# Interleaving the slots of two expert tiles by retrieval rounds in a hybrid encoder layer on one Trainium2 core

## The chip, the cores and the metric

The kernel runs on one core of one Trainium2 chip. The metric is the device time of one execution in microseconds. The median of three runs of the kernel before is 1806.68 us (1801.11 to 1808.39).

## The reference

One layer of a streaming encoder for 640 tokens of 1024 channels: 128 tokens of eight running streams and 512 of a prompt, all in float32. In the kernel these are five tiles of 128 tokens; tile 0 holds the running streams, tiles 1 to 4 the prompt. After the mixing front (a gMLP half and an RG-LRU half), each token asks for experts:

```python
q = (xb @ w_q).reshape(PEER_BLOCK, PEER_HEADS, 2, D_HALF)      # 8 heads, 2 halves of 128
s1 = einsum("thd,kd->thk", q[:, :, 0], k1); s2 = einsum("thd,kd->thk", q[:, :, 1], k2)
v1, i1 = top_k(s1, 16); v2, i2 = top_k(s2, 16)
cand = v1[..., :, None] + v2[..., None, :]                     # best 16 of the pair sums
top_s, sel = top_k(cand, 16); eidx = take_along_axis(cidx, sel); g = softmax(top_s)
act = gelu(einsum("thkd,td->thk", u_tab[eidx], xb))
y = einsum("thk,thkd->td", g * act, v_tab[eidx])
```

So each token has 8 x 16 = 128 experts out of 16384, each a row of u_tab (1024 numbers) and one of v_tab. The host lays the two tables side by side as `experts`, 8 KB a row. The result is added to x, and a last RMSNorm gives y.

## The kernel before, in words

**A slot** is one expert for each of a tile's 128 tokens: one indirect DMA of POOL. The sparse tiles 0, 3 and 4 gather whole rows, u and v (1 MB a slot). For the dense tiles 1 and 2 only u rows are gathered (0.5 MB, `udot`), and their v part is a product with the whole v table: two table passes over it, each of 64 blocks of 128 rows (0.5 MB, loaded by SP at L585). Before each pass a filling builds the matrix of coefficients `cm` of the pass for all 256 dense tokens, in 32 batches of 8 tokens: VectorE compares (`one_hot`, L1030 and L1032), ScalarE scales (L1296), TensorE multiplies (`fill`, L1556), ScalarE copies (L1304). The pass is `add_block`, L1567.

**A whole slot** goes: gather (L631), dot with h2 on VectorE (`dot`, L969), gelu and coefficient on ScalarE (L1266, L1270). Then its v row is added: either on TensorE, with a diagonal made by ScalarE (L1277) and four matmul records into accY (`weigh`, L1582), or on VectorE (`add_v`, L989). `by_vector` (L181) says which. Tile 3 is on TensorE in its first 64 slots, tile 4 in three of five; both are on VectorE in the other 64, which run beside a table pass. `take` (L1050) adds accY to the tile, after its last slot.

**The ring** has six places of 8 KB per partition, twelve half places for u rows. POOL issues the gathers in the order of the dots (`GATHERS`), each after the ring place's last user is done (`freed`) and, at each new retrieval round, after `idx_ready` (L625).

**Retrieval.** The queries of tiles 3 and 4 are made in 8 rounds, one head each (`Q` items, L1500); ScalarE keeps them (L1261). A round then goes in steps x: scores on TensorE at x = 5r + 4, best keys at 5r + 5 and 5r + 6, pair sums at 5r + 7, second eight at 5r + 8, numbers and weights at 5r + 9, all but the scores on VectorE (L840 to L959). A round gives 16 slots to each of the two tiles.

**The order** of all engines is one list, `ORDER`. `weave` (L87) gives each item a due number and sorts by it; each engine walks the list and executes its part in that order. Due numbers are about microseconds of the plan, not measured ones. After the dots of tile 0 and the u rows of tile 1 come the front of tiles 3 and 4 beside the u rows of tile 2, then filling and pass with tile 3, then filling and pass with tile 4. `adopt` (L999) makes h2 of the next tile, `ids` and `prep` bring the dense tiles' numbers and coefficients to the layout of the filling, `flush` (L1042) adds a pass's result, `norm` and `square_y` are the last RMSNorm.

## Time and profile before

| | |
|---|---|
| median of three runs | 1806.68 us |
| those runs, lowest and highest | 1801.11, 1808.39 us |
| profiled execution, span | 1799.8 us (its time with what lies around the span is not listed) |
| TensorE busy | 1455.5 us, 81% |
| VectorE busy | 1429.5 us, 79% |
| ScalarE busy | 634.6 us, 35% |
| POOL busy | 801.6 us, 45% |
| DMA | 675.75 MB, mean 375 GB/s |
| whole-slot gathers, u gathers | 384, 256 |
| dots L969 | 466.4 us in 384, 1222 ns each |
| adds on VectorE L989 | 238.3 us in 186, 1281 ns each |

The page's busy shares are means over stages with different limits. The slices (40 of 45 us) show the stages; the windows, groups, waits and timelines below are of the same execution. A busy time counts an instruction from start to end, and neighbours overlap a little: where a cost is wanted, the distance between starts is the better measure.

### The profile page before, as it was taken

The numbers are of one execution on the slowest core, as the hardware profiler recorded it, in microseconds if no ns is written. First come the engines' busy times: TensorE is split into PE (matmuls) and PEld (weight loads), VectorE is DVE, ScalarE is ACT, GpSimd is POOL, SyncE is SP. The second block draws the span as 40 slices with busy tenths as digits, with TensorE's granted clock in tenths as the row PEclk, the third lists the DMA queues.
The fourth block names the chain that finished last, engine by engine and source line by source line (L and its number), as shares of the span: only waits on it lengthen the run. The fifth ranks groups of instructions, "written<-read, shape, count | busy, mean of one in ns | idle before, by whom it ended". The sixth has DMA issues, their size and how long they took to land.

```text
span 1799.8 us, 16917 instructions
## 1 busy us (share of the span) xinstructions
PE 1455.5 (81%) x4706; PEld 790.5 (44%) x4706; DVE 1429.5 (79%) x3050; ACT 634.6 (35%) x1936; POOL 801.6 (45%) x667
## 2 busy tenths in 40 slices
...
GB/s 355 155 342 409 384 358 402 341 396 398 408 398 410 379 415 397 386 342 392 405 304 307 353 345 362 418 416 417 416 417 352 371 351 375 388 417 417 417 417 283
DMA packets 146478, 675.75 MB, mean 375 GB/s; under 512 B 15216, under 2 KB 15472, under 8 KB 97232
## 3 DMA queue, kind: packets, MB, share of 16 engines
...
HBM read 671.61 MB, written 3.01 MB: 375 GB/s over the span
## 4 chain that ended last, share of the span: by engine, by line
DMA 28%; PE 27%; DVE 16%; issue 10%; POOL 9%; ACT 8%; ACTq 0%; DVEq 0%; POOLq 0%; SPq 0%
DMA ring<-experts,idc 19%; DMA arena<-experts 9%; PE accY L1582 8%; POOL ring L633 8%; PE pb L1567 5%; PE pb L1373 4%; DVE ring L969 3%; DVE ring L980 3%; PE pb L1382 2%; PE pb L1556 2%; ACT arena L1296 2%; POOL ring L631 2%; DVE xt L989 2%; DVE arena L1030 2%; PE pb L1391 1%
## 5 line engine op out<-in xcount | busy, mean ns | idle before, releaser
L631 POOL DMA_INDIRECT ring<-experts,idc x384 | 462.7, 1205 | 844.4 <-DVE xt L989 373.6
L969 DVE CUSTOM_DVE_ANT_0 ring<-ring,h 128x1024 f32<-128x1024 f32 x384 | 466.4, 1222 | 198.0 <-DMA ring<-experts,idc 196.7
L1582 PE MATMUL accY<-ring,diag 128*128 128x512 f32 x792 | 450.4, 704 | 197.0 <-ACT diag L1277 197.0
L1567 PE MATMUL pb<-arena 128*128 128x512 f32 x1024 | 472.4, 606 | 19.7 <-DMA arena<-experts 13.1
L633 POOL DMA_INDIRECT ring<-experts,idc x256 | 328.7, 1284 | 110.5 <-issue 76.3
L1266 ACT ACTIVATE ge<-zt 128x1 f32<-128x1 f32 x384 | 76.4, 199 | 757.8 <-DVE zt L969 756.4
L1582 PEld LDWEIGHTS accY<-ring,diag 128*128 128x128 f32 x792 | 157.6, 216 | 402.9 <-ACT diag L1277 275.0
L1567 PEld LDWEIGHTS pb<-arena 128*128 128x128 f32 x1024 | 186.1, 191 | 304.4 <-issue 197.4
L989 DVE SCALAR_TENSOR_TENSOR xt<-ring,coef,xt 128x1024 f32<-128x1024 f32 x186 | 238.3, 1281 | 14.2 <-ACT coef L1270 13.9
L980 DVE CUSTOM_DVE_ANT_0 ring<-ring,h 128x1024 f32<-128x1024 f32 x128 | 151.7, 1222 | 8.3 <-DMA ring<-experts,idc 7.2
L1296 ACT ACTIVATE arena<-arena,qT 128x64 f32<-128x64 f32 x512 | 129.1, 334 | 81.2 <-DVE arena L1032 81.2
L980 DVE CUSTOM_DVE_ANT_0 ring<-ring,arena 128x1024 f32<-128x1024 f32 x128 | 153.2, 1221 | 5.5 <-DMA ring<-experts,idc 4.7
L1500 PE MATMUL pq<-arena 128*128 128x256 f32 (+1 forms) x736 | 147.6, 359 | 7.3 <-ACT arena L1261 3.9
L1556 PEld LDWEIGHTS pb<-arena 128*128 128x128 f32 x1024 | 131.3, 201 | 41.7 <-issue 31.2
L1500 PEld LDWEIGHTS pq<-arena 128*128 128x128 f32 x736 | 128.0, 199 | 32.7 <-issue 18.6
L1556 PE MATMUL pb<-arena 128*128 128x64 f32 x1024 | 127.6, 280 | 4.8 <-ACT arena L1296 4.8
L1270 ACT ACTIVATE coef<-ge,gc 128x1 f32<-128x1 f32 x384 | 113.1, 295 | 12.6
L1030 DVE TENSOR_TENSOR arena<-iota,qT 128x1024 f32<-128x1024 f32 x64 | 78.2, 1222 | 20.7 <-PE pb L1556 20.7
L1277 ACT ACTIVATE diag<-ident,coef 128x128 f32<-128x128 f32 x198 | 79.5, 402 | 6.4
L1363 PE MATMUL pb<-ident,arena 128*128 128x128 f32 x100 | 18.5, 355 | 72.8 <-ACT arena L1124 52.2
L1373 PE MATMUL pb<-arena 128*128 128x256 f32 (+1 forms) x384 | 72.7, 352 | 2.9 <-ACT arena L1131 2.9
L1382 PE MATMUL pb<-arena 128*128 128x512 f32 x144 | 66.1, 616 | 6.3 <-ACT arena L1173 6.3
...
## 6 DMA issues: line engine op xcount, KB each, us to landing
arena<-experts SPq DMA_DIRECT2D x128, 512.0 KB, 15.0
...
ring<-experts,idc POOLq DMA_INDIRECT x640, 9.5
...
```

The source lines that it names most:

```text
L631: nc.gpsimd.indirect_dma_start(ring[:, at // 2], None, experts, index).then_inc(gat[at], 16)
L633: nc.gpsimd.indirect_dma_start(half(g), None, halves, index).then_inc(gat[at], 16)
L969: V.tensor_tensor_reduce(out=half(g), in0=half(g), in1=h2[:], scale=1.0, scalar=0.0, op0=ALU.mult, op1=ALU.add, accum_out=zt[:, s % 8:s % ...
L980: V.tensor_tensor_reduce(out=half(g), in0=half(g), in1=h, scale=1.0, scalar=0.0, op0=ALU.mult, op1=ALU.add, accum_out=zd[:, u:u + 1]).then ...
L989: V.scalar_tensor_tensor(out=x, in0=ring[:, PLACE["whole", s][0] // 2, D:2 * D], scalar=coef[:, s % 8:s % 8 + 1], in1=x, op0=ALU.mult, op1 ...
L1030: V.tensor_tensor(hot2[:, k % 2], iota[:].unsqueeze(1).to_broadcast([P, BATCH, P]), idT[:, 1, a].unsqueeze(2).to_broadcast([P, BATCH, P]), ...
L1296: ins = A.activation(hot1[:, k % 2, i], hot1[:, k % 2, i], ACT.Copy, scale=idT[:, 2, n * BATCH + i:n * BATCH + i + 1])
L1373: ins = T.matmul(pflat[:, o:o + w], wt[:, c, m * P:(m + 1) * P], hT[:, c, 0:w], start=c == 0, stop=c == DC - 1)
L1500: ins = T.matmul(out, wt[:, c, o:o + P], h2T[:, c, 0:w], start=c == 0, stop=c == DC - 1)
L1556: ins = T.matmul(pb[:, k % 4, i * BLOCKS:(i + 1) * BLOCKS], hot2[:, k % 2, i], hot1[:, k % 2, i], start=True, stop=True)
L1567: ins = T.matmul(pb[:, 2 * j + k], cm[:, i, j * P:(j + 1) * P], vring[:, n % VRING, k * 512:(k + 1) * 512], start=i == 0, stop=i == BLOCKS ...
L1582: ins = T.matmul(accY[:, j], diag[:, (n - 1) % DIAGS], ring[:, place, D + j * 512:D + (j + 1) * 512], start=first, stop=final)
```

## The change

The slots of tiles 3 and 4 no longer run tile by tile. `slot_order` lists them: 24 of tile 3 (the tail) between the last u rows and a little beyond; the first filling with 54 (24 of tile 3, 30 of tile 4); the first pass with 62 (18 of tile 4, 44 of tile 3); the second filling with 54 (36 of tile 3, 18 of tile 4); the second pass with 62 of tile 4. In the tail all slots are on TensorE, in the fillings four of five, in the passes none. Rounds 0 to 2 of the retrieval are due in the tail's stretch, rounds 3 to 7 all in the first pass. Tile 3's h2 lies in a tensor of its own, h3, in the place of the gate weights, so that both tiles can be dotted in any order; tile 4's is made in h2 after the last u row. The accumulation on TensorE is cut into runs of one tile (`RUNS`): a take stands after each run, and the next run's first weighing waits for it. There are five runs where there were three. The last RMSNorm's square is an item of its own, since a tile is complete only after its last slot. `adds_before` and `takes_before` count adds ahead of takes and takes ahead of adds, for their waits.

```diff
-SPARSE = [0, 3, 4]
+TAIL, FILLED, BLOCKED = 24, 54, 62
+
+def slot_order():
+
+    third = [(3, k) for k in range(SLOTS)]
+    fourth = [(4, k) for k in range(SLOTS)]
+    tail = third[0:24]
+    fill0 = third[24:48] + fourth[0:30]
+    block0 = fourth[30:48] + third[48:92]
+    fill1 = third[92:128] + fourth[48:66]
+    block1 = fourth[66:128]
+    assert (len(tail), len(fill0), len(block0), len(fill1), len(block1)) == (TAIL, FILLED, BLOCKED, FILLED, BLOCKED)
+    return [(0, k) for k in range(SLOTS)] + tail + fill0 + block0 + fill1 + block1
+
+SLOT = slot_order()
+WHOLE = len(SLOT)
+
+def stretch(s):
+
+    at = s - SLOTS - TAIL
+    if at < 0:
+        return ("first", s) if s < SLOTS else ("tail", s - SLOTS)
+    half, at = divmod(at, FILLED + BLOCKED)
+    return ("fill", at) if at < FILLED else ("block", at - FILLED)
+
+def by_vector(s):
+
+    kind, i = stretch(s)
+    if kind == "first":
+        return i < SLOTS // 2 and i % 2 == 1
+    return kind == "block" or (kind == "fill" and i % 5 == 3)
+
+ON_PE = [sum(not by_vector(k) for k in range(s + 1)) for s in range(WHOLE)]
+ON_DVE = [s + 1 - ON_PE[s] for s in range(WHOLE)]
+LAST_SLOT = {t: max(s for s in range(WHOLE) if SLOT[s][0] == t) for t in (0, 3, 4)}
+
+def runs_on_pe():
+
+    runs = []
+    for s in range(WHOLE):
+        if not by_vector(s):
+            if not runs or SLOT[runs[-1][-1]][0] != SLOT[s][0]:
+                runs.append([])
+            runs[-1].append(s)
+    return runs
+
+RUNS = runs_on_pe()
+RUN_OF = {s: g for g, run in enumerate(RUNS) for s in run}
...
             u += 1
     b += 0.6
     put.append((b + 2.02, ("take", 0)))
+    put.append((b + 2.03, ("square", 0)))
...
     for r in range(HEADS):
         for part in range(3):
-            put.append((b + 55.04 + 0.9 * (3 * r + part), ("Q", r, part)))
-    for x in range(4, 10):
-        put.append((b + 58.08 + 2.6 * (x - 4), ("II", 2, x)))
+            put.append((b + 55.04 + 1.2 * (3 * r + part), ("Q", r, part)))
+    c = b + 55.0
+    for x in range(4, 20):
+        put.append((c + 3.58 + 2.2 * (x - 4), ("II", 2, x)))
+    put.append((c + 6.11, ("adopt", 3)))
+    s = SLOTS
+    for n in range(TAIL):
+        put.append((c + 15.61 + 1.2 * n, ("dot", s + n)))
+        put.append((c + 16.72 + 1.2 * n, ("mix", s + n)))
     while u < DTOK:
-        b += 0.6
-        put.append((b, ("udot", u)))
-        u += 1
-    b += 1.0
-
-    for x in range(10, rounds_steps(2)):
-        r, k = divmod(x - 10, 5)
-        put.append((b - 3 + 16 * r + 2.7 * k + 0.07, ("II", 2, x)))
+        wide = 1.2 if b < c + 14 else 2.4
+        for _ in range(2):
+            put.append((b, ("udot", u)))
+            u += 1
+        b += wide
     put.append((b - 12.01, ("ids",)))
-    put.append((b + 0.02, ("adopt", 3)))
     put.append((b + 0.2, ("prep",)))
-    s = SLOTS
+    put.append((b + 0.4, ("adopt", 4)))
+
+    b = c + 15.61 + 1.2 * TAIL
+    s += TAIL
+    taken = 1
     for h in range(2):
-        for n in range(64):
+        hot = (FILLED - 2) / BATCHES
+        for n in range(FILLED):
             put.append((b + 0.1 + n, ("dot", s + n)))
             put.append((b + 1.11 + n, ("mix", s + n)))
         for n in range(BATCHES):
-            put.append((b + 1.5 + 1.9 * n, ("hot", h, n)))
-            put.append((b + 3.55 + 1.9 * n, ("fill", h, n)))
-        b += 64
-        for n in range(64):
-            put.append((b + 0.1 + 1.5 * n, ("dot", s + 64 + n)))
-            put.append((b + 1.61 + 1.5 * n, ("mix", s + 64 + n)))
+            put.append((b + 0.5 + hot * n, ("hot", h, n)))
+            put.append((b + 2.45 + hot * n, ("fill", h, n)))
+        for g, run in enumerate(RUNS):
+            if g >= taken and s <= run[-1] < s + FILLED:
+                put.append((b + 1.61 + run[-1] - s, ("take", g)))
+                taken = g + 1
+        if h == 1:
+            put.append((b + 4.0 + LAST_SLOT[3] - s, ("square", 3)))
+            put.append((b + 7.02 + LAST_SLOT[3] - s, ("norm", 3)))
+        b += FILLED
+        s += FILLED
+        wide = 1.5 * BLOCKS / BLOCKED
+        for n in range(BLOCKED):
+            put.append((b + 0.1 + wide * n, ("dot", s + n)))
+            put.append((b + 1.61 + wide * n, ("mix", s + n)))
         for n in range(BLOCKS):
             put.append((b + 0.7 + 1.5 * n, ("block", h, n)))
+        if h == 0:
+            for x in range(20, rounds_steps(2)):
+                put.append((b + 1.33 + 2.6 * (x - 20), ("II", 2, x)))
         b += 96
-        s += SLOTS
+        s += BLOCKED
         if h == 0:
-            put.append((b + 0.05, ("adopt", 4)))
-            put.append((b + 0.4, ("take", 3)))
             put.append((b + 1.3, ("flush", 0)))
-            put.append((b + 5.02, ("norm", 3)))
-    put.append((b + 2.0, ("take", 4)))
+    put.append((b + 2.0, ("square", 4)))
     put.append((b + 2.1, ("norm", 4)))
     put.append((b + 2.2, ("flush", 1)))
     put.append((b + 2.3, ("norm", 1)))
...
-def by_vector(s):
-
-
-    t, k = divmod(s, SLOTS)
-    if t == 0:
-        return k < SLOTS // 2 and k % 2 == 1
-    return k >= SLOTS // 2 or (t == 2 and k % 5 in (1, 3))
-
-
-WHOLE = len(SPARSE) * SLOTS
-ON_PE = [sum(not by_vector(k) for k in range(s + 1)) for s in range(WHOLE)]
-ON_DVE = [s + 1 - ON_PE[s] for s in range(WHOLE)]
...
         ws = sb("ws", [GROUPS, P])
-        wab = sb("wab", [HC, P])
-        wib = sb("wib", [HC, P])
+        wabi = sb("wabi", [2 * HC, P])
+        wab = wabi[:, 0:HC]
+        wib = wabi[:, HC:2 * HC]
+        h3 = wabi[:].rearrange("p m n -> p (m n)")
...
+            known = 0
             for g in GATHERS:
                 kind, s = g
                 at, _, lay = PLACE[g]
-                t, k = SPARSE[s // SLOTS] if kind == "whole" else DENSE[s // SLOTS], s % SLOTS
+                t, k = SLOT[s] if kind == "whole" else (DENSE[s // SLOTS], s % SLOTS)
                 f = FRONT_OF[t]
                 per = SLOTS // ROUNDS[f]
-                if k % per == 0 or (f == 0 and k == TOPK):
-                    first = f == 0 and k == 0
-                    pool.wait_ge(idx_ready, 1 if first else ROUND_BASE[f] + k // per + 2)
+                ready = 1 if f == 0 and k < TOPK else ROUND_BASE[f] + k // per + 2
+                if ready > known:
+                    pool.wait_ge(idx_ready, ready)
                     pool.sem_inc(pool_held, 1)
+                    known = ready
                 if lay:
                     freed(pool, lay)
...
             def dot(s):
-                g = "whole", s
-                if s % SLOTS == 0:
-                    v.wait_ge(h2_ready, H2_TILES.index(SPARSE[s // SLOTS]) + 1)
+                g, t = ("whole", s), SLOT[s][0]
+                if all(tile != t for tile, _ in SLOT[:s]):
+                    v.wait_ge(h2_ready, H2_TILES.index(t) + 1)
-                V.tensor_tensor_reduce(out=half(g), in0=half(g), in1=h2[:], scale=1.0, scalar=0.0, op0=ALU.mult,
...
             def add_v(s):
-                t = SPARSE[s // SLOTS]
-                x = xt[:, X_PLACE[t]]
+                x = xt[:, X_PLACE[SLOT[s][0]]]
                 v.wait_ge(coefs, s + 1)
+                if s and TAKES_AT_ADD[s] and by_vector(s):
+                    v.wait_ge(y_taken, TAKES_AT_ADD[s])
...
                 if t == 4:
-                    v.wait_ge(dots, 2 * SLOTS)
-                V.scalar_tensor_tensor(out=h2[:], in0=xt[:, X_PLACE[t]], scalar=rs_ffn[:, t:t + 1], in1=g_ffn[:],
+                    v.wait_ge(udots, DTOK)
+                V.scalar_tensor_tensor(out=h3 if t == 3 else h2[:], in0=xt[:, X_PLACE[t]], scalar=rs_ffn[:, t:t + 1], in1=g_ffn[:],
                                        op0=ALU.mult, op1=ALU.mult).then_inc(h2_ready, 1)
...
-            def take(t):
-                n = SPARSE.index(t)
-                x = xt[:, X_PLACE[t]]
-                v.wait_ge(vdone, ON_PE[SLOTS * (n + 1) - 1])
-                v.wait_ge(vadds, ON_DVE[SLOTS * (n + 1) - 1])
+            def take(g):
+                x = xt[:, X_PLACE[SLOT[RUNS[g][-1]][0]]]
+                v.wait_ge(vdone, ON_PE[RUNS[g][-1]])
+                v.wait_ge(vadds, ADDS_AT_TAKE[g])
                 V.tensor_tensor(x, x, accY[:].rearrange("p a b -> p (a b)"), ALU.add).then_inc(y_taken, 1)
...
             def square_y(t):
                 n = LAST.index(t)
-                a.wait_ge(y_taken, n + 1)
+                if t in DENSE:
+                    a.wait_ge(y_taken, len(RUNS) + DENSE.index(t) + 1)
+                else:
+                    a.wait_ge(y_taken, max(g for g, run in enumerate(RUNS) if SLOT[run[-1]][0] == t) + 1)
+                    a.wait_ge(vadds, ON_DVE[LAST_SLOT[t]])
...
-                n, k = ON_PE[s], s % SLOTS
-                first = k == 0
-                final = not any(not by_vector(o) for o in range(s + 1, s - k + SLOTS))
-                if first and s:
-                    t.wait_ge(y_taken, s // SLOTS)
+                n, run = ON_PE[s], RUN_OF[s]
+                first, final = s == RUNS[run][0], s == RUNS[run][-1]
+                if first and run:
+                    t.wait_ge(y_taken, run)
```

## Rows read from the trace of the kernel before

**Rows 1.** The page, slices: GB/s that DMA moved in each of 40 slices.
```profile
GB/s 355 155 342 409 384 358 402 341 396 398 408 398 410 379 415 397 386 342 392 405 304 307 353 345 362 418 416 417 416 417 352 371 351 375 388 417 417 417 417 283
```

**Rows 2.** Windows: busy us (instructions) of each engine, then PEclk, DMA share, GB/s.
```profile
855.00:919.00 64.00, 52.26 (x235) 44.10 (x234) 60.32 (x172) 7.52 (x14) 41.27 (x33) 0.95 1.00 387
919.00:1115.00 196.00, 178.46 (x799) 110.18 (x800) 179.54 (x444) 146.26 (x509) 81.52 (x62) 0.97 0.89 332
1115.00:1357.00 242.00, 231.59 (x516) 93.33 (x514) 184.57 (x347) 41.74 (x147) 66.55 (x65) 0.99 1.02 414
1357.00:1545.00 188.00, 153.76 (x681) 99.36 (x681) 166.07 (x222) 125.23 (x457) 88.45 (x63) 0.88 0.94 359
1545.00:1799.80 254.80, 236.61 (x514) 92.24 (x512) 163.53 (x202) 37.34 (x138) 58.06 (x60) 0.99 0.96 393
```

**Rows 3.** Timeline of VectorE: start us, duration us, line, operation.
```profile
891.66 0.50 DVE L840 MAX8 best<-pick 128x8 f32<-128x136 f32 x2
...
894.99 1.22 DVE L980 CUSTOM_DVE_ANT_0 ring<-ring,h 128x1024 f32<-128x1024 f32 x1
...
899.57 1.22 DVE L901 TENSOR_REDUCE e<-pick 128x64 f32<-128x1024 f32 x1
...
901.23 1.22 DVE L980 CUSTOM_DVE_ANT_0 ring<-ring,h 128x1024 f32<-128x1024 f32 x1
...
908.10 0.50 DVE L840 MAX8 vals<-psc 128x8 f32<-128x128 f32 x2
...
910.59 1.21 DVE L980 CUSTOM_DVE_ANT_0 ring<-ring,h 128x1024 f32<-128x1024 f32 x1
...
925.87 0.19 DVE L860 TENSOR_TENSOR pick<-vals 128x32 f32<-128x32 f32 x1
...
928.14 1.22 DVE L969 CUSTOM_DVE_ANT_0 ring<-ring,h 128x1024 f32<-128x1024 f32 x1
...
929.28 1.22 DVE L1030 TENSOR_TENSOR arena<-iota,qT 128x1024 f32<-128x1024 f32 x1
...
931.02 1.22 DVE L969 CUSTOM_DVE_ANT_0 ring<-ring,h 128x1024 f32<-128x1024 f32 x1
```

**Rows 4.** The same, at the start of the second filling.
```profile
1364.83 2.35 DVE L1042 TENSOR_TENSOR xt<-xt,pb 128x1024 f32<-128x1024 f32 x2 [4.88 <-PE pb L1567]
...
1369.98 1.28 DVE L989 SCALAR_TENSOR_TENSOR xt<-ring,coef,xt 128x1024 f32<-128x1024 f32 x1
```

**Rows 5.** Waits in the first filling: us in total, times, longest.
```profile
DVE arena L1030 <- PE pb L1556: 11.9, 7, 3.1
```

**Rows 6.** Waits in the second filling, 1375 to 1545 us.
```profile
PE accY L1582 <- ACT diag L1277: 23.9, 11, 3.6
...
DVE arena L1030 <- PE pb L1556: 8.8, 6, 2.2
...
DVE xt L989 <- ACT coef L1270: 4.7, 8, 0.7
```

**Rows 7.** Timeline of TensorE in the first filling.
```profile
1005.43 3.65 PE L1582 MATMUL accY<-ring,diag 128*128 128x512 f32 x8
1008.92 1.89 PE L1556 MATMUL pb<-arena 128*128 128x64 f32 x16
```

**Rows 8.** Groups of VectorE from 855 to 919 us: count, busy, mean ns.
```profile
L980 DVE CUSTOM_DVE_ANT_0 ring<-ring,h 128x1024 f32<-128x1024 f32 x36 | 42.6, 1221 | 3.2 <-DMA ring<-experts,idc 2.9
```

**Rows 9.** Timeline at the first gather of the kernel.
```profile
98.70 0.17 DVE L933 SCALAR_TENSOR_TENSOR idc<-e 128x16 int32<-128x16 f32 x1
...
109.28 1.23 DVE L969 CUSTOM_DVE_ANT_0 ring<-ring,h 128x1024 f32<-128x1024 f32 x1
```

**Rows 10.** Timeline of TensorE: one query round of tiles 3 and 4.
```profile
861.61 7.14 PE L1500 MATMUL pq<-arena 128*128 128x256 f32 x32 [0.78 <-ACT arena L1261]
```

**Rows 11.** Timeline of ScalarE: back from Sqrt to Gelu.
```profile
1361.61 1.28 ACT L1266 ACT_TABLE_LOAD   x1
...
1362.90 0.20 ACT L1266 ACTIVATE ge<-zt 128x1 f32<-128x1 f32 x1
```

29 lines of the change are left out of this document (24 added, 5 removed).

## The prediction

> **What bounds the kernel now.** I read the page's slices first. DMA moves about 417 GB/s in the two stretches of five slices or so that are the table passes, and 303 to 376 GB/s in most slices of the two stretches that are the fillings [rows 1]. So the ceiling here is 417 GB/s: the whole traffic, 675.75 MB by the page, would take 1620 us at it, and the span is 1799.8 us. The kernel loses 180 us in which DMA isn't full. Then I cut the end of the run by stage [rows 2]: u rows of tile 2 (855 to 919 us), filling of tile 3 (919 to 1115), first pass (1115 to 1357), filling of tile 4 (1357 to 1545), second pass and end (1545 to 1799.8). The passes run at 414 GB/s and, with the end in it, 393; the fillings at 332 and 359. At 417 GB/s a whole slot (1.049 MB) costs 2.515 us, a u row half of it, 1.257, a block of the table 1.257. A filling of 64 slots needs 161 us of DMA; the first takes 196 and the second 188. These 35 and 27 us are what the change can win; the 91 us or so lost before 855 us it leaves alone.
>
> What holds the fillings is VectorE, in its order. From starts of neighbouring instructions [rows 3]: a dot takes 1.14 to 1.15 us, a pair of one-hots 1.74, and one retrieval round 2 x 2.49 (best keys) + 2.27 (sums) + 3.33 + 1.66 = 12.2 us; a vector add 1.28 at most [rows 4]. First filling: 64 x 1.147 + 32 x 1.74 + about 3.5 rounds x 12.2 = 73 + 56 + 43 = 172, busy 180 of 196. Second: 73 + 56 + 26 adds x 1.2 + 5 for take, norm and flush = 165, busy 166 of 188 [rows 2]. There the rest are short waits: one-hots for TensorE's filling 8.8 us, adds for their coefficient 4.7 [rows 6]; in the first filling the former are 11.9 [rows 5]. TensorE needs 3.49 / 2 = 1.745 us for a slot, start to start, and for a batch of filling 1.89 less an overlap of 0.16, 1.73 [rows 7]: 112 + 55 = 167 us in the first filling, 66 + 55 = 121 in the second.
>
> **The change, stage by stage.** Up to c, the point 92 u rows into tile 2, nothing in the order moves but the squares' name. 36 u rows run in 855 to 919 [rows 8], so c is at 855 us on VectorE.
>
> (1) From c to the first tail slot. Round 0 now ends (x 9) at due c + 14.58, after 24 u rows; two more u rows and the first tail dot (c + 15.61) follow. VectorE: 24 x 1.147 + 12.2 + 1.3 for adopting tile 3 = 41 us, so the numbers are ready at about 896. But the gathers are issued in the order of the dots by a queue that waits in line: the gather of tail slot 0 needs idx_ready of round 0, and its ring slot is free 12 half slots earlier, at due c + 8.6. From there to the numbers VectorE has 8 u rows and x 7 to 9: 9.2 + 7.3 = 16.5 us in which POOL, and all u gathers behind it, is held. This is a new wait. What is in flight (at most the ring's twelve half places; I estimate 9 u rows, 9 x 1.257) drains in about 12 us of it; then DMA is idle for some 5 us and 2 more until bytes flow: 7 us lost (bounds: 0 if weight pieces fill the hole, 16.5). The nearest row for what follows is the kernel's first gather: from idc at 98.70 to the first dot at 109.28 are 10.6 us with six gathers queued [rows 9]. The first tail dot is thus at about 906.
>
> By the Trainium skill (DMA: Bandwidth & Descriptors, Anatomy of one DMA) a gather takes some 2.0 us plus its bytes at 436 GB/s, 4.4 us here, so an estimate by it would put that dot 5 us earlier; the row differs, and it decides.
>
> (2) The tail: 24 slots with 10 u rows, rounds 1 and 2, ids, prep and the adoption of tile 4. VectorE: 34 x 1.147 + 24.4 + 4 = 67.5. DMA: 24 x 2.515 + 10 x 1.257 = 73, begun at 898. TensorE: 24 x 1.745 = 42, and of the eight query rounds only 0 to 4 stand ahead of the first tail weighing in its order; 5 to 7 come between them at 7.14 + 0.78 = 7.92 us each [rows 10], 24 us, and scores and turns 4: 70. All three would end at 971 to 976. They are coupled through six ring slots, so I add 4: the tail ends at **979** (970 to 990). Against the kernel before, 24 slots and their 60 us of DMA are out of the fillings.
>
> (3) First filling, now 54 slots, no rounds, 11 adds on VectorE. DMA 54 x 2.515 = 136. VectorE 61.9 + 55.7 + 11 x 1.2 + 2 takes 2.4 = 133. TensorE 43 x 1.745 + 55.4 = 130. ScalarE was busy 125 us in the second filling [rows 2], with as many batches, 10 more slots and 5 fewer diagonals: again some 125. Nothing is late by itself, but four queues within 8% of each other don't run without gaps: the stalls of [rows 5, 6] stay. I take 11.9 for one-hots (as where TensorE was as full as here), 2 for 11 adds, 3 for each take in the middle (VectorE waits for TensorE's last weighing of the run, and TensorE's first of the next for y_taken; no row shows it; 0 to 4). That is 133 + 17 = **150 us** (139 to 165). Of 196 before, 46 go, but 10 slots' worth, 25, return in the tail.
>
> (4) First pass: 62 slots, 64 blocks. DMA 62 x 2.515 + 64 x 1.257 = 236. The five rounds 3 to 7 lie here. Before, the last rounds already ran in this pass at 414 GB/s [rows 2]. VectorE: 62 x (1.147 + 1.28) + 61 = 212, under 236, so rounds cost next to nothing; if that cover went they would cost up to 61. Numbers of round 3 come at slot 7 and their first slot is gathered at slot 12. Of 242 before, two slots (5) go and 1 comes: **238** (236 to 250).
>
> (5) Second filling: as the first, but with the wait for TensorE's end of the pass (4.9 us [rows 4]), flush, square and norm of tile 3 in its middle. VectorE 61.9 + 55.7 + 13.2 + 2.4 + 1.5 + 2.3 = 137; stalls 17 + 4.9: **158** (147 to 172). The square's Sqrt takes two table loads, one 1.28 us [rows 11]: 4 us on ScalarE in the middle of work that has only 10 free; contained in that range.
>
> The Trainium skill (ScalarE: Activation LUTs, What ACT_TABLE_LOAD costs) adds a drain of 1.38 us to the load's 1.28, an estimate of 2.8 us more for the two; in the trace the Gelu starts at 1362.90, right behind its load [rows 11], so the load agrees and no drain is seen.
>
> (6) Second pass and end: 254.8 less two slots, 5, less the last take, 1: **249** (247 to 253).
>
> Sum: 979 + 150 + 238 + 158 + 249 = 1774 us of span, 26 less than 1799.8. The time around the span isn't shown on the page; the median of the three runs, 1806.68, is 6.9 above the span, and I keep that distance: 1781, said as **1780 us**.
>
> **Rivals.**
> A, the fillings run at DMA's pace: stalls hide in the ring, since now DMA is the longest queue. For it: in the second filling DMA already ran at 359 with VectorE 2% over it. Then no loss at the hold, 971 + 139 + 238 + 143 + 249 = 1740, time 1747.
> B, slower: TensorE becomes the bound of the fillings. It had 38 weighings to 32 batches in the second filling and still waited 23.9 us for the diagonal [rows 6], with its clock at 0.88 [rows 2]; with 43 in a shorter filling the same 0.63 us per weighing (27) and the same clock (130 / 0.88 = 148) give 175 a filling: 979 + 175 + 238 + 182 + 249 = 1823, time 1830. It decides once the two fillings together pass 334 us. Against it: in the first filling TensorE, busy 178 of 196, held 0.97 of the clock [rows 2].
> C, no gain: the hold of POOL comes with every round (0, 1, 2), not only the first, and each costs DMA 10 us: 1774 + 20 = 1794, time 1801. Against it: round 1 is due 2 slots ahead of its gather's turn, and round 2 further.
>
> **Chances.** Forecast 0.5; A 0.26; C 0.12; B 0.12. The range is to hold 8 in 10: it reaches down to A's time, about which half of A lies above, and up over C's 1801, **1746 to 1808**. A measurement of this kernel can tell about 0.5%, 9 us, from no change. Faster by more than that (under 1797.6): the forecast, A and a little of C, 0.77; within it 0.11; slower (over 1815.7) 0.12.
>
> **What would show it.** The GB/s row of the page should lie at 370 or more through the fillings, and the fillings last 150 and 158 us. Rounds 3 to 7 (L843, L901) should stand inside the first pass, with DMA still at 410 or more. Around 890 us a POOL gather should wait some 15 us for idc, with a dip in GB/s. In fillings the waits of the one-hots (L1030 before) for TensorE should be 10 us or so each, those of a take 1 to 4. Step 4 is wrong if the first pass exceeds 250; step 3 if TensorE's waits for the diagonal pass 25 us in a filling. The prediction fails as a whole if DMA loses time before 855 us, which I hold unchanged.

## The result, and the profile after

The kernel after the change takes 1820.1 us (median of 11 runs, 1808.3 to 1826.43); the kernel before, on the same chips, 1807.64 us (11 runs, 1798.14 to 1810.19). The ratio is 1.0072, with an interval from 1.0054 to 1.0089: slower by 0.7%, where 1780 us and a range up to 1808 us had been forecast. The profiled execution has a span of 1818.7 us, 18.9 longer than the one before (12.5 by the medians), and 44.7 longer than the 1774 us of the sum.

The page's slices of the kernel after, GB/s that DMA moved in each of 40 (45.5 us each); they answer to [rows 1]:

```profile
GB/s 350 154 356 408 378 379 402 339 393 395 408 392 411 387 411 357 395 328 405 310 388 395 345 338 326 380 416 406 387 414 408 330 367 327 351 418 417 417 416 255
```

The two table passes are the runs of slices from 387 to 418. Before the first come a slice of 310 (POOL is held in it), two of 388 and 395 (the tail) and four of 326 to 380 (the first filling); the second filling's four stand at 327 to 367. In the fillings 370 or more had been named as the mark of a right forecast. The windows by stage, with the columns of [rows 2]: c to the first tail dot, the tail of 24 slots, first filling, first pass, second filling, second pass and end.

```profile
855.00:906.00 51.00, 34.46 (x151) 28.58 (x149) 45.48 (x119) 5.53 (x10) 24.18 (x24) 0.87 0.84 325
906.00:988.00 82.00, 69.39 (x213) 39.56 (x214) 67.87 (x199) 31.62 (x91) 42.40 (x35) 0.96 0.98 385
988.00:1158.00 170.00, 146.94 (x686) 95.66 (x684) 132.88 (x185) 118.42 (x439) 73.65 (x54) 0.93 0.91 344
1158.00:1404.00 246.00, 233.72 (x549) 104.08 (x549) 214.78 (x505) 50.84 (x168) 96.21 (x63) 0.96 1.01 408
1404.00:1570.00 166.00, 146.38 (x683) 96.09 (x683) 130.61 (x181) 118.53 (x430) 74.25 (x53) 0.91 0.92 337
1570.00:1818.70 248.70, 234.79 (x511) 92.92 (x509) 163.82 (x196) 36.35 (x134) 60.48 (x58) 0.99 0.94 386
```

Set against the sum: the first tail dot was forecast at 906 us and stands at 906.13. The tail takes 82 us instead of 73, the first filling 170 instead of 150, the first pass 246 instead of 238, the second filling 166 instead of 158, the end 248.7 instead of 249. The differences are +9, +20, +8, +8 and 0, together the 45 us. In the two fillings VectorE is busy 133 and 131 us, close to its forecast work (133 and 137), and idle for the rest; DMA runs at 344 and 337 GB/s. So the work was counted nearly rightly, and the stalls weren't.

Where VectorE idles in the first filling (988 to 1158 us) is told by the groups of its lines: count, busy us, mean ns, then idle time ahead of them with what ended it.

```profile
L1120 DVE TENSOR_TENSOR arena<-iota,qT 128x1024 f32<-128x1024 f32 x32 | 39.1, 1223 | 24.5 <-PE pb L1649 24.5
L1058 DVE CUSTOM_DVE_ANT_0 ring<-ring,h 128x1024 f32<-128x1024 f32 x31 | 37.1, 1220 | 1.1 <-DMA ring<-experts,idc 1.1
...
L1079 DVE SCALAR_TENSOR_TENSOR xt<-ring,coef,xt 128x1024 f32<-128x1024 f32 x10 | 12.8, 1282 | 1.8 <-ACT coef L1359 1.8
...
L1139 DVE TENSOR_TENSOR xt<-xt,accY 128x1024 f32<-128x1024 f32 x2 | 2.4, 1220 | 8.8 <-PE accY L1674 8.8
```

The one-hots of L1120 wait 24.5 us for the filling matmuls of L1649; the two takes of L1139 wait 8.8 us for TensorE's weighings (1.7 us the one in the middle, 7.2 us the one at the filling's end); dots lose 3.2 us to gathers and adds 1.8 to coefficients. The sum of all idle rows is 38.3 us, and 131.7 + 38.3 = 170. The waits of both fillings (us in total, times, longest), first filling first, then two rows of the second:

```profile
PE accY L1674 <- ACT diag L1366: 21.6, 14, 2.5
...
DVE arena L1120 <- PE pb L1649: 22.8, 13, 4.0
PE accY L1674 <- ACT diag L1366: 19.5, 11, 3.0
```

And the same view over the whole run:

```profile
DVE arena L1120 <- PE pb L1649: 47.3, 27, 4.1
...
DVE xt L1139 <- PE accY L1674: 19.5, 4, 7.8
```

The one-hots waited 20.7 us in 13 places in the whole run before (its two fillings are in [rows 5, 6]); now it is 47.3 in 27.

The hold of POOL, as timelines (start us, duration us): the last gather ahead of it and the first tail gather on POOL, then the numbers and the first tail dot on VectorE.

```profile
880.54 0.94 POOL L722 DMA_INDIRECT ring<-experts,idc  x1 [0.30 <-issue]
900.11 1.44 POOL L720 DMA_INDIRECT ring<-experts,idc  x1 [18.63 <-DVE idc L1036]
...
899.11 0.19 DVE L1036 SCALAR_TENSOR_TENSOR idc<-e 128x32 int32<-128x32 f32 x1
...
906.13 1.23 DVE L1058 CUSTOM_DVE_ANT_0 ring<-ring,wabi 128x1024 f32<-128x1024 f32 x1 [4.24 <-issue]
```

POOL stands 18.63 us for the numbers of L1036 (16.5 forecast). The dot follows 7.0 us behind the numbers, where [rows 9] had 10.6, and 6.0 us behind the gather that starts at 900.11. By the Trainium skill (DMA: Bandwidth & Descriptors, Anatomy of one DMA) this gather would take an estimated 4.4 us; the 6.0 us of this row lie between that and the row I had chosen, and decide.

In the tail (906 to 988 us) the waits are these:

```profile
POOL ring L720 <- PE accY L1674: 33.8, 17, 5.5
...
DVE ring L1058 <- DMA ring<-experts,idc: 11.8, 11, 1.9
...
DVE ring L1058 <- issue: 4.2, 1, 4.2
```

POOL waits 33.8 us for weighings to free a ring slot, while VectorE waits for gathered data: the coupling through six slots for which I had added 4 us.

### The profile page after: what moved, and what is told of

The parts are those of the page before. It is cut to its first block, busy times and chain, and to the rows that moved or that the text cites. A ratio compares the mean times of both kernels' runs of the same rounds, so it can differ in the third digit from the quotient of the medians.

```text
span 1818.7 us, 16965 instructions
## 1 busy us (share of the span) xinstructions
PE 1472.1 (81%) x4738; PEld 810.7 (45%) x4738; DVE 1426.7 (78%) x3044; ACT 637.3 (35%) x1944; POOL 832.4 (46%) x667
## 4 chain that ended last, share of the span: by engine, by line
PE 31%; DMA 20%; DVE 18%; issue 12%; ACT 10%; POOL 9%; ACTq 0%; DVEq 0%; POOLq 0%
DMA ring<-experts,idc 11%; PE accY L1674 11%; DMA arena<-experts 9%; POOL ring L722 7%; PE pb L1660 5%; DVE ring L1058 4%; PE pb L1466 4%; PE pb L1649 3%; ACT arena L1385 3%; PE pb L1475 2%; DVE ring L1069 2%; DVE xt L1079 2%; PE pq L1593 2%; ACT coef L1359 1%; POOL ring L720 1%
## 5 line engine op out<-in xcount | busy, mean ns | idle before, releaser
L720 POOL DMA_INDIRECT ring<-experts,idc x384 | 495.9, 1291 | 826.2 <-PE accY L1674 368.4
L1674 PE MATMUL accY<-ring,diag 128*128 128x512 f32 x824 | 475.8, 714 | 203.3 <-ACT diag L1366 203.1
L1660 PE MATMUL pb<-arena 128*128 128x512 f32 x1024 | 461.7, 604 | 10.1 <-DMA arena<-experts 7.1
L1058 DVE CUSTOM_DVE_ANT_0 ring<-ring,h 128x1024 f32<-128x1024 f32 x256 | 311.0, 1222 | 86.5 <-DMA ring<-experts,idc 85.7
L722 POOL DMA_INDIRECT ring<-experts,idc x256 | 326.2, 1274 | 109.7 <-issue 76.9
L1674 PEld LDWEIGHTS accY<-ring,diag 128*128 128x128 f32 x824 | 167.2, 219 | 424.4 <-ACT diag L1366 274.4
L1660 PEld LDWEIGHTS pb<-arena 128*128 128x128 f32 x1024 | 191.7, 192 | 277.1 <-issue 223.6
L1079 DVE SCALAR_TENSOR_TENSOR xt<-ring,coef,xt 128x1024 f32<-128x1024 f32 x178 | 228.3, 1282 | 74.4 <-ACT coef L1359 74.2
L1058 DVE CUSTOM_DVE_ANT_0 ring<-ring,wabi 128x1024 f32<-128x1024 f32 x128 | 154.9, 1220 | 23.8 <-DMA ring<-experts,idc 19.4
L1069 DVE CUSTOM_DVE_ANT_0 ring<-ring,h 128x1024 f32<-128x1024 f32 x128 | 151.9, 1223 | 7.7 <-DMA ring<-experts,idc 6.8
L1649 PEld LDWEIGHTS pb<-arena 128*128 128x128 f32 x1024 | 130.8, 201 | 33.3 <-issue 32.8
L1649 PE MATMUL pb<-arena 128*128 128x64 f32 x1024 | 126.5, 280 | 0.0
L1120 DVE TENSOR_TENSOR arena<-iota,qT 128x1024 f32<-128x1024 f32 x64 | 78.3, 1223 | 47.3 <-PE pb L1649 47.3
L1366 ACT ACTIVATE diag<-ident,coef 128x128 f32<-128x128 f32 x206 | 82.7, 402 | 6.8
L1466 PE MATMUL pb<-arena 128*128 128x256 f32 (+1 forms) x384 | 76.5, 365 | 2.9 <-ACT arena L1220 2.9
## 6 DMA issues: line engine op xcount, KB each, us to landing
arena<-w_q SPq DMA_DIRECT2D x12, 2048.0 KB, 18.9
```

What stands on the lines that cost most here:

```text
L720: nc.gpsimd.indirect_dma_start(ring[:, at // 2], None, experts, index).then_inc(gat[at], 16)
L722: nc.gpsimd.indirect_dma_start(half(g), None, halves, index).then_inc(gat[at], 16)
L1058: V.tensor_tensor_reduce(out=half(g), in0=half(g), in1=h3 if t == 3 else h2[:], scale=1.0, scalar=0.0, op0=ALU.mult, op1=ALU.add, accum_ou ...
L1069: V.tensor_tensor_reduce(out=half(g), in0=half(g), in1=h, scale=1.0, scalar=0.0, op0=ALU.mult, op1=ALU.add, accum_out=zd[:, u:u + 1]).then ...
L1079: V.scalar_tensor_tensor(out=x, in0=ring[:, PLACE["whole", s][0] // 2, D:2 * D], scalar=coef[:, s % 8:s % 8 + 1], in1=x, op0=ALU.mult, op1 ...
L1466: ins = T.matmul(pflat[:, o:o + w], wt[:, c, m * P:(m + 1) * P], hT[:, c, 0:w], start=c == 0, stop=c == DC - 1)
```

## The experiments

Each edit is made on the kernel after, unless it says "on the kernel before". Ratios are against the kernel before, with their 95% intervals; the kernel after stands at 1.0072 [1.0054, 1.0089]. "One-hot waits" are the waits of L1120 for L1649 over the whole run. Two sizes of the order by hand are needed below. The distance between batches is 1.625 dues after ((FILLED - 2) / BATCHES) and 1.9 before. The lag is how long after its one-hots a filling is due: 2.45 - 0.5 = 1.95 after, 3.55 - 1.5 = 2.05 before.

### A third pair of one-hot buffers: e1_third_hot

```diff
-        hot2 = part(16384, 2048).rearrange("p (b k n) -> p b k n", b=2, k=BATCH)
-        hot1 = part(18432, 1024).rearrange("p (b k n) -> p b k n", b=2, k=BATCH)
+        hot2 = [part(a, 1024).rearrange("p (k n) -> p k n", k=BATCH) for a in (16384, 17408, 20224)]
...
+        hot1 = [part(18432, 512).rearrange("p (k n) -> p k n", k=BATCH),
+                part(18944, 512).rearrange("p (k n) -> p k n", k=BATCH),
+                part(19456, 512).rearrange("p (k n) -> p k n", k=BATCH)]
...
-                    sp.wait_ge(filled, BATCHES * (n // BLOCKS + 1) if n % VRING < 3 else 1)
+                    sp.wait_ge(filled, BATCHES * (n // BLOCKS + 1))
...
-                if k >= 2:
-                    v.wait_ge(filled, k - 1)
+                if k >= 3:
+                    v.wait_ge(filled, k - 2)
```

> The changed kernel with three pairs of one-hot buffers where there were two (the third in free space and over the stage's dead part); the first block of the second pass is loaded a little later for it. Theory T (one-hots wait for TensorE's filling because only two buffers stand between them; these waits were 24.5 and 22.8 us in the two fillings of the changed kernel): the waits fall under 5 us each, the fillings go from 170 and 166 us to about 150, the time from 1820 to about 1785. Theory P (TensorE has too much in a filling, the one-hots' wait is only where that shows): the wait moves to the dots or the ring, the fillings stay within 5 us, time 1815 to 1820.

The cuts hold only the change from `k % 2` to `k % 3` where the buffers are used. The third pair lies over space that the table's first blocks use, so these wait for the whole filling (the edit at `sp.wait_ge`). 1781.02 us, ratio 0.9866 [0.9834, 0.9898]. Its windows, first filling, first pass, second filling:

```profile
985.00:1133.00 148.00, 134.66 (x686) 89.64 (x684) 131.84 (x182) 117.74 (x439) 72.82 (x54) 1.00 0.99 394
1133.00:1375.00 242.00, 226.91 (x546) 102.11 (x547) 212.65 (x503) 48.72 (x160) 96.02 (x64) 0.98 1.01 411
1375.00:1525.00 150.00, 139.95 (x683) 92.32 (x682) 132.22 (x184) 120.31 (x439) 68.82 (x53) 0.95 0.96 373
```

The fillings take 148 and 150 us, the stalls on one-hots are gone, and the kernel is 1.3% faster than before where it had been 0.7% slower. TensorE, with the same instructions, is busy 135 us instead of 147, at a granted clock of 1.00 instead of 0.93. Breaking the wait for the second buffer gives the loss back, with all the work left in place.

### The last take of a filling later: e2_late_take

```diff
-                put.append((b + 1.61 + run[-1] - s, ("take", g)))
+                put.append((b + 1.61 + run[-1] - s + (3.0 if run[-1] - s > FILLED - 3 else 0), ("take", g)))
```

> The changed kernel with the take at the end of each filling due 3 slots later, so that VectorE goes on with dots and adds of the pass while TensorE ends its weighings. Theory K (the new takes drain the engines; VectorE stood 7.2 and 7.8 us before these two): both waits vanish and the time falls by up to 15 us, to 1805. Theory T or P (what counts is TensorE's backlog; in these 7 us DMA was going on): the waits vanish and the time stays within 4 us of 1820.

1813.74 us, ratio 1.0048 [1.0024, 1.0072]. The takes' waits fall from 19.5 to 3.1 us, those of the one-hots only from 47.3 to 43.5. The interval overlaps that of the kernel after, so the gain of some 4 us (by the ratios; 6 by the medians) isn't shown, only that it is under about 12.

### Round 0 in one go: e3_early_round0

```diff
-        put.append((c + 3.58 + 2.2 * (x - 4), ("II", 2, x)))
+        put.append((c + 3.58 + (1.0 if x < 10 else 2.2) * (x - 4), ("II", 2, x)))
```

> The changed kernel with the steps of retrieval round 0 due 1.0 apart instead of 2.2, so that its numbers come at due c + 8.6, before POOL's turn at the first tail gather. Theory H (the hold of POOL, 18.6 us, costs DMA some 7 to 12 us): the wait for the numbers falls under 5 us, DMA in 855 to 906 us rises from 325 to above 370 GB/s, and the time falls by 7 to 10 us, to 1811. If the tail is bound by TensorE's queries anyway: the tail's end doesn't move, time 1820.

1810.21 us, ratio 1.0034 [1.0015, 1.0053], just apart from that of the kernel after: the hold costs about 7 us by the ratios, which is what I had put down. (The medians differ by 10, but the kernel before was also 3 us faster beside this run.) The window from c to the first tail dot:

```profile
855.00:906.00 51.00, 34.81 (x138) 26.92 (x137) 50.23 (x142) 7.81 (x17) 30.65 (x24) 0.84 0.99 378
```

DMA moves 378 GB/s there instead of 325, and POOL's long wait is gone. The waits of the one-hots stay at 47.6 us.

### Two slots in five on VectorE: e4_two_in_five

```diff
-    return kind == "block" or (kind == "fill" and i % 5 == 3)
+    return kind == "block" or (kind == "fill" and i % 5 in (1, 3))
```

> The changed kernel with two of five slots of the fillings added on VectorE instead of one: 32 or 33 weighings for TensorE in each filling in place of 43, and 11 more adds of 1.2 us on VectorE. Theory P (TensorE's load is what holds the fillings): TensorE has 18 us less, fillings 170 and 166 go to about 155, time about 1795. Theory T (buffers and order): the one-hots' wait falls by half, VectorE's load rises to 146, fillings about 163, time 1810. Theory V (VectorE's order is the bound as in the kernel before): fillings 180, time 1840.

1818.91 us, ratio 1.0081 [1.0054, 1.0108]: no gain. The first filling:

```profile
989.00:1162.00 173.00, 143.01 (x642) 96.47 (x640) 144.88 (x195) 114.98 (x428) 75.89 (x54) 0.84 0.88 331
```

Eleven weighings left TensorE and it is busy only 4 us less, with its clock at 0.84 instead of 0.93; VectorE got 12 us more to do. The one-hot waits fell to 30.8 us over the run and the filling still took 173. (The profiled execution is this run's slowest, 1828.93 us, so the window may be a few us long.) No theory's time was met: 1795 and 1810 were too low, 1840 too high. Taking load off TensorE is thus no remedy here, but the run doesn't say that its load is innocent either, because the clock changed with it.

### The third pair on the kernel before: e5_before_third_hot

The same edit as in e1, on the kernel before.

> The kernel before with three pairs of one-hot buffers in place of two, its order untouched. Its one-hots waited 11.9 and 8.8 us for TensorE in the two fillings. Theory T (the buffers matter as far as the wait for them is long): these 21 us go, but the first filling stays bound by VectorE's own 172 us of work, so the time falls by 8 to 18 us, to 1790 or 1797, far less than the 39 us that the same edit gave the changed kernel. If both kernels gain 35 us or more, the changed order is worth no more than before and the buffers alone are the whole story.

1795.4 us, ratio 0.9933 [0.9902, 0.9965]; one-hot waits 0.4 us instead of 20.7. The old order was losing by the same wait, with less than half the waits and, by the ratios, 12 us of time where the new one loses 37. With the third pair on both sides the new order is the faster one: 0.9866 against 0.9933, intervals apart. So the change of order is worth 12 us (by the ratios) to 14 us (by the medians) by itself, as long as the one-hots don't wait.

### The filling sooner behind its one-hots: e6_fill_sooner

```diff
-            put.append((b + 2.45 + hot * n, ("fill", h, n)))
+            put.append((b + 1.55 + hot * n, ("fill", h, n)))
```

> The changed kernel with two pairs of buffers, but TensorE's filling of a batch due 1.05 after its one-hots in place of 1.95, so 0.9 slots sooner in TensorE's order; nothing else moves. Theory T as order (a one-hot waits since the filling two batches back stands behind weighings in TensorE's line): the waits of 24.5 and 22.8 us fall by half or more, fillings to about 158, time 1798. Theory T as buffers alone (the round through VectorE, ScalarE, TensorE is too long for two): waits within 5 us of what they were, because TensorE now waits for ScalarE's scaling instead, time 1815 to 1822.

1785.65 us, ratio 0.9891 [0.9848, 0.9934], with two buffers only. One-hot waits 3.7 us instead of 47.3; fillings 148 and 152 us. What the number 2.45 did is seen in the timeline of the kernel after (start us, duration us; each instruction's idle time and releaser in brackets):

```profile
1062.28 1.22 DVE L1120 TENSOR_TENSOR arena<-iota,qT 128x1024 f32<-128x1024 f32 x1
...
1064.02 1.22 DVE L1058 CUSTOM_DVE_ANT_0 ring<-ring,h 128x1024 f32<-128x1024 f32 x1
...
1064.13 2.02 ACT L1385 ACTIVATE arena<-arena,qT 128x64 f32<-128x64 f32 x8 [1.97 <-DVE arena L1122]
...
1066.06 0.19 ACT L1355 ACTIVATE ge<-zt 128x1 f32<-128x1 f32 x1
...
1066.60 0.40 ACT L1366 ACTIVATE diag<-ident,coef 128x128 f32<-128x128 f32 x1
...
1067.06 3.55 PE L1674 MATMUL accY<-ring,diag 128*128 128x512 f32 x4 [1.07 <-ACT diag L1366]
...
1070.40 2.06 PE L1649 MATMUL pb<-arena 128*128 128x64 f32 x16
...
1072.50 1.23 DVE L1120 TENSOR_TENSOR arena<-iota,qT 128x1024 f32<-128x1024 f32 x1 [2.08 <-PE pb L1649]
```

The one-hots of a batch start at 1062.28. Their scaling on ScalarE, 1064.13 to 1066.15, stands ahead of the gelu of a dot that had ended by 1065.2; so the diagonal (L1366) comes at 1066.60, and TensorE's weighing, which had waited 1.07 us for it, starts at 1067.06. It takes 3.55 us instead of 1.95: the granted clock from 1067.0 to 1070.6 us is 0.55, so nearly all of it ran at the lower of the two levels (1.2 instead of 2.4 GHz). The filling of the batch, whose inputs had been ready since 1066.15, is behind that weighing in TensorE's order and starts at 1070.40. The one-hots two batches on need its buffer: they start at 1072.50, after 2.08 us of waiting, and every dot of VectorE is behind them. Some 16 us later it happens again: the weighing at 1082.98 has waited 1.74 us for its diagonal.

The low clock is a part of this ring. In the first filling the five longest of the 14 one-hot waits, 2.08 to 4.09 us and 14.3 of the 24.5 us together, stand right behind a weighing that had waited 1.07 to 2.06 us for its diagonal and then took 2.48 to 3.55 us. Against 1.95 us for a weighing and 1.89 for a filling these five places lost 9 us to the clock. So TensorE waits, is then slower, and the filling behind it is later still. No run holds the clock fixed, so how long the waits would be without this isn't known. The same place in e6:

```profile
1064.41 1.22 DVE L1120 TENSOR_TENSOR arena<-iota,qT 128x1024 f32<-128x1024 f32 x1
...
1066.26 2.02 ACT L1385 ACTIVATE arena<-arena,qT 128x64 f32<-128x64 f32 x8 [0.72 <-DVE arena L1122]
...
1066.76 1.94 PE L1674 MATMUL accY<-ring,diag 128*128 128x512 f32 x4
...
1068.44 1.22 DVE L1120 TENSOR_TENSOR arena<-iota,qT 128x1024 f32<-128x1024 f32 x1
...
1068.53 1.89 PE L1649 MATMUL pb<-arena 128*128 128x64 f32 x16
...
1071.32 1.22 DVE L1120 TENSOR_TENSOR arena<-iota,qT 128x1024 f32<-128x1024 f32 x1
```

Scaling 1066.26, weighing 1066.76 at 1.94 us, filling right behind it at 1068.53, and neither of the next one-hots (1068.44, 1071.32) waits.

### All three edits, and the rounds spread: e7_all_three, e8_rounds_spread

e7 is e1, e2 and e3 together. e8 adds:

```diff
-                put.append((b + 1.33 + 2.6 * (x - 20), ("II", 2, x)))
+                put.append((b + 1.33 + 3.4 * (x - 20), ("II", 2, x)))
```

> The changed kernel with the third pair of buffers, the later takes and the early round 0 together. If the three losses are separate they add: 1781 less 6 less 9 is 1766. If they stand for the same slack, 1775 to 1781.

> As e7, with the steps of rounds 3 to 7 due 3.4 apart over the whole first pass in place of 2.6. In the changed kernel the pass ran at 408 GB/s, VectorE busy 215 of 246 us. If the density of the rounds costs the pass its 5 us: GB/s in the pass rises to 415 and the time falls by 3 to 5 us from e7. If not, the time is that of e7 within 2 us.

e7: 1782.03 us, 0.9862 [0.9817, 0.9908]; e8: 1784.42 us, 0.9867 [0.9823, 0.991]. Neither is apart from e1. The first two windows of e7, c to the first tail dot and the tail:

```profile
855.00:905.00 50.00, 35.65 (x162) 30.04 (x160) 49.20 (x127) 6.05 (x13) 31.36 (x25) 0.90 1.00 387
905.00:985.00 80.00, 70.69 (x211) 39.17 (x212) 64.83 (x194) 30.80 (x89) 41.40 (x34) 0.91 0.94 359
```

What is won up to 905 us (387 GB/s) is given back in the tail (359 instead of 385), and its first filling takes 154 us instead of the 148 of e1. The small gains of e2 and e3 don't add to that of e1.

### The sooner filling on the kernel before: e9_before_sooner

```diff
-            put.append((b + 3.55 + 1.9 * n, ("fill", h, n)))
+            put.append((b + 2.65 + 1.9 * n, ("fill", h, n)))
```

> The kernel before with TensorE's filling of a batch due 1.15 after its one-hots in place of 2.05. Its slack (the due distance from a filling to the one-hots two batches on, which wait for it) goes from 1.75 to 2.65. Theory S (this slack in the order sets the wait): the waits of 11.9 and 8.8 us go, time as with three buffers, about 1795; so the changed order with the same edit (1785.7) is then really faster than the old one, by 8 to 12 us.

1791.89 us, 0.9916 [0.9884, 0.9949]; one-hot waits 6.4 us. It agrees with e5: the old order has this stall too, and gains some 15 us when it goes (0.84% of 1808). Its interval overlaps that of e6, so what the new order is worth by itself rests on e1 against e5.

### Third pair, sooner filling and early round 0: e10_third_sooner_early

> The changed kernel with three pairs of buffers, the filling sooner and round 0 early, takes as in the change. Theory S: with the one-hots' wait already gone the sooner filling adds nothing: 1778 to 1783. If TensorE's place of the filling has a worth of its own: under 1775.

1783.45 us, 0.9864 [0.9826, 0.9901], one-hot waits 0.9 us. Where one of the remedies has removed the wait, the other has nothing left to win.

### The filling later: e11_fill_later, e12_before_later

e11, on the kernel after:

```diff
-            put.append((b + 2.45 + hot * n, ("fill", h, n)))
+            put.append((b + 2.95 + hot * n, ("fill", h, n)))
```

e12, on the kernel before:

```diff
-            put.append((b + 3.55 + 1.9 * n, ("fill", h, n)))
+            put.append((b + 4.00 + 1.9 * n, ("fill", h, n)))
```

> The changed kernel with two buffers and the filling due 2.45 after its one-hots in place of 1.95: slack 0.8 for 1.3. Theory S: the one-hots' waits grow from 47 to 75 us or more for both fillings together, fillings 182 each, time 1840 to 1850. If the slack doesn't matter: 1820.

> The kernel before with the filling due 2.50 after its one-hots in place of 2.05: slack 1.3, as in the changed kernel. Theory S: its one-hots' waits go from 21 us to 30 or 40 and the time to 1815 or 1825. If the changed kernel's waits come from TensorE's load rather than from the slack, the time stays within 5 us of the kernel before.

e11: 1816.91 us, 1.0066 [1.0044, 1.0088]. e12: 1805.65 us, 0.9986 [0.9958, 1.0013], one-hot waits 23.2 us where they had been 20.7. The first filling of e11, and its one-hot waits over the whole run:

```profile
988.00:1148.00 160.00, 141.92 (x681) 94.55 (x680) 131.45 (x183) 117.24 (x436) 74.70 (x53) 0.95 0.94 354
...
DVE arena L1120 <- PE pb L1649: 47.7, 33, 6.4
```

I had held by then that the wait grows steadily with the lag; on the later side it doesn't. In e11 it stays at 47.7 us, only split into 33 waits instead of 27, and the filling is 10 us shorter, for all that the median doesn't move (the profiled execution is this run's fastest, 1811.14 us). That theory fell. What would fit is a step: it matters whether the filling comes ahead of the next batch's one-hots in the order by hand, not how far behind them.

### Half the columns in a filling's weighings: f1_half_weighing

```diff
+                w = 512 if first or final or stretch(s)[0] != "fill" else 256
...
-                    ins = T.matmul(accY[:, j], diag[:, (n - 1) % DIAGS], ring[:, place, D + j * 512:D + (j + 1) * 512],
+                    ins = T.matmul(accY[:, j, 0:w], diag[:, (n - 1) % DIAGS], ring[:, place, D + j * 512:D + j * 512 + w],
```

> The changed kernel, two buffers, with weighings in the fillings that add only half of the columns (256 of each 512), except a run's first and last: part of the v rows of tiles 3 and 4 is left out. TensorE has some 35 us less in each filling. Theory P (TensorE's load): the one-hots' waits of 47 us fall under 10 and the time to 1785 or less. Theory L (the round one-hots, scaling, filling behind weighings that wait for their diagonal is what takes long, not the weighings' own time): waits fall by less than half, time above 1800.

1826.32 us, 1.0113 [1.0092, 1.0135]; one-hot waits 49.2 us. The first filling:

```profile
988.00:1158.00 170.00, 139.51 (x683) 121.19 (x684) 131.62 (x182) 115.89 (x429) 69.96 (x52) 0.76 0.91 344
```

This kernel leaves half of the columns out of nearly all the fillings' weighings, and TensorE is still busy 139.5 us of 170: its granted clock is 0.76 instead of 0.93. So the load wasn't halved in time, and the run can't tell what a truly lighter TensorE would bring. It does show, as e4 did, that leaving TensorE less to do in these fillings doesn't shorten them, at the clock that is then granted.

### Half of the scalings: f2_half_scaling

```diff
-                for i in range(BATCH):
+                for i in range(0, BATCH, 2):
```

> The changed kernel, two buffers, with only four of the eight one-hots of a batch scaled by their coefficient: part of the dense tiles' coefficients is left out. ScalarE's step between one-hots and filling takes 1.0 us for 2.0, and its queue is 32 us shorter in each filling. Theory L: each round is 1 us shorter, the waits fall by half and more and the time to 1790 or 1800. Theory P: waits and time stay, 1815 to 1820.

1781.42 us, 0.9863 [0.9842, 0.9883]. The first filling, and the one-hot waits of the whole run:

```profile
988.00:1136.00 148.00, 136.03 (x686) 90.08 (x684) 131.27 (x182) 90.02 (x311) 76.99 (x54) 0.99 0.99 391
...
DVE arena L1120 <- PE pb L1649: 16.0, 17, 2.5
```

This kernel leaves half of the one-hots unscaled. ScalarE is busy 90 us instead of 118, on an engine that had 50 us free; yet the filling falls from 170 to 148 us. The scaling stands ahead of two things in the timeline above: of the filling that needs it, and of the gelu and diagonal behind it on ScalarE. This run shortens both and doesn't tell them apart, but it shows that this link belongs to the ring.

### The filling just ahead of the next one-hots: f3_fill_a_bit_sooner

```diff
-            put.append((b + 2.45 + hot * n, ("fill", h, n)))
+            put.append((b + 2.00 + hot * n, ("fill", h, n)))
```

> The changed kernel, two buffers, filling due 1.50 after its one-hots in place of 1.95, where 1.05 had removed the wait; the distance of batches is 1.625, so the filling now stands ahead of the next batch's one-hots instead of behind them. If that place is what counts (theory O): waits under 12 us, time 1785 to 1792. If the wait falls evenly with the distance: about half of 47 us, time 1800 to 1805.

1783.76 us, 0.9862 [0.9835, 0.989]. First filling, first pass, second filling, and the one-hot waits:

```profile
988.00:1139.00 151.00, 139.13 (x687) 90.54 (x685) 132.73 (x184) 118.22 (x439) 73.91 (x54) 0.98 0.97 382
1139.00:1385.00 246.00, 232.20 (x548) 101.31 (x548) 215.29 (x506) 50.85 (x168) 96.19 (x64) 0.98 1.01 412
1385.00:1533.00 148.00, 138.90 (x682) 92.75 (x683) 130.69 (x181) 118.57 (x430) 73.47 (x53) 0.96 0.95 373
...
DVE arena L1120 <- PE pb L1649: 10.5, 13, 2.1
```

A lag of 1.50 is just under the batches' distance of 1.625, so each filling comes in the order ahead of the next batch's one-hots, and with it ahead of some of the weighings around them. This smallest step takes the one-hot waits to 10.5 us and has the whole gain of the large one (e6). It is the simplest version that beats both kernels: one number. Before had the lag (2.05) over the distance (1.9) as well, which fits with e9's gain. The step isn't shown to be the mechanism, though: TensorE's queue holds no one-hots, and the edit also takes weighings out from between a batch's one-hots and its filling. Counted in `ORDER` there are 1.56 of them on average in the kernel after, 1.19 in f3, 0.81 in e6 and 1.94 in e11. Place and count move together in f3; that e11 has more weighings there and no longer wait speaks for the place.

## Why the prediction was wrong, point by point

**Bound and counts: right in the main.** The first pass runs at 408 GB/s (411 and 412 in e1 and f3). VectorE's work in a filling is 133 and 131 us (133 and 137 forecast), ScalarE's 118 (125). TensorE's is 135 us at full clock (e1; 130 forecast), but 147 and 146 at the clock that it was granted. The last stage, 248.7, was forecast at 249. Before c the kernel is some 3 us late: the 221st u row's dot starts at 856.90 us, before at 853.85.

**Step 1, the hold: right, its end by luck.** POOL was held 18.6 us against 16.5, and the cost is that forecast, about 7 us (e3). The numbers came at 899.1 instead of 896, and the dot 7.0 us behind them instead of 10.6: two errors that cancel to 906.

**Step 2, the tail: 9 us short.** 82 us, at 385 GB/s. The rows show POOL waiting for weighings and VectorE for gathers. How much of the 9 is the query rounds between the weighings and how much the ring, no run separates; it stays open. It lasts 79 us in e1 as well, where the one-hots never wait, so most of it isn't part of their matter.

**Step 3, the first filling: this is the step that failed, and with it step 5.** The mechanism had been named: one-hots wait for TensorE's filling. Its size was taken over from before, 11.9 us [rows 5], with the reason that TensorE was as full there. It measured 24.5 us in the first filling and 22.8 in the second. The sum had one take in each filling, the one in the middle, at 3 us: it measured 1.7 and 2.9. It put the wait of the take at the filling's end at nothing, without a reason: 7.2 and 7.8 us, of which the time shows little (e2). With 3 us of waits for gathers, for which the sum had nothing either, the stalls of the first filling are 38.3 us instead of 17. Those of the second are 35.4 instead of 21.9; with 131 us of work they make its 166 (a few of the 137 us lie ahead of the window).

The row that I had chosen depended on where the filling stood among one-hots, scalings and weighings, and the change altered just that: batches 1.625 apart instead of 1.9, with nearly the same lag. I read that edit as a matter of amounts (32 batches are 32 batches) and never wrote the four queues down side by side for one batch. "Four queues within 8% of each other don't run without gaps" was the right unease with no price worked out for it. The sign that I had given for step 3, waits for the diagonal over 25 us, didn't show (21.6 and 19.5): it looked at another place than the one where the time went.

Any of three kinds of edit that break the ring brings the fillings to within 1 us of their forecast or under it: a third buffer (fillings 148 and 150 us, 1781.02 us), the filling ahead of the next one-hots (151 and 148 us, 1783.76 us), a shorter scaling (148 us for the first, 1781.42 us). That the ring of waits is the cause is shown by these; how it divides into waiting and lower clock isn't. The forecast was 150 and 158 us, 1780 in all, and that e1 comes within 1 us of 1780 is partly luck. Its tail, first pass and end are 6, 4 and 4.5 us over the sum. Its fillings are 10 us under it together, and 5 more were put too high for the time around the span.

Why a distance of 1.625 makes twice the wait of 1.9, when in both kernels the filling stands behind the next one-hots, and why a still later filling does no harm (e11, e12), isn't shown.

**Step 4, the first pass: 8 us short, and VectorE had lost its cover.** 246 us, also in f3, where the fillings are short; so it isn't the ring. The forecast held 212 us of VectorE's work against 236 of DMA. VectorE is busy 215 us, and the waits of the pass, which the sum had at nothing, take most of what was left:

```profile
DVE xt L1079 <- ACT coef L1359: 22.7, 38, 0.6
...
1394.96 1.23 DVE L1058 CUSTOM_DVE_ANT_0 ring<-ring,wabi 128x1024 f32<-128x1024 f32 x1 [0.67 <-DMA ring<-experts,idc]
...
1396.79 1.28 DVE L1079 SCALAR_TENSOR_TENSOR xt<-ring,coef,xt 128x1024 f32<-128x1024 f32 x1 [0.60 <-ACT coef L1359]
```

The same place in the kernel before, where no add of the pass waits for its coefficient:

```profile
1343.62 1.23 DVE L969 CUSTOM_DVE_ANT_0 ring<-ring,h 128x1024 f32<-128x1024 f32 x1 [1.33 <-DMA ring<-experts,idc]
...
1344.77 1.28 DVE L989 SCALAR_TENSOR_TENSOR xt<-ring,coef,xt 128x1024 f32<-128x1024 f32 x1
```

This too is the order by hand. Before, slots of a pass were due 1.5 apart, so the add of slot n (1.61 + 1.5n) stood behind the dot of slot n + 1 (1.6 + 1.5n). The change spread them to 1.55 (`wide`), and the add now stands ahead of the next dot, right behind its own, and waits 0.60 us for gelu and coefficient. With 6.7 us of waits for gathers that makes 244 of the 246 us. The second pass has 36.5 us of such waits and still took its forecast time; it has no retrieval rounds. So rounds and waits together are the likely reason of the 8 us, but no run puts the old order back. Spreading the rounds (e8) won nothing, and e1 and e7 have 242 and 239.

**Rival B came true in its sum and in most of its terms, but not in its cause.** The two fillings took 336 us, just over the 334 given as the point from which it decides. TensorE was busy 147 us and waited 21.6 for the diagonal in the first filling, 146 and 19.5 in the second (148 and 27 assumed for each), with the clock at 0.93 and 0.91 (0.88): that is 168.5 of 170 and 165.9 of 166 us. But the amount of its work was not the bound: in e1, e6 and f3 it has the same instructions and the fillings take 148 to 152 us; in e4 and f1 it has less to do and the first takes 173 and 170. Its lower clock is there with the stalls and mostly gone without them (0.95 to 1.00 in e1, e6 and f3). **Rival A** (stalls hide in the ring) and **rival C** (the hold at every round) are out: DMA ran at 337 to 344 GB/s in the fillings, and only round 0 holds POOL.

**The time around the span** was taken as 6.9 us and is 1.9 in the profiled execution (1820.62 against 1818.7): the 6.9 had set the median against the span of a faster execution.
